# Filler products on TensorE inside the router of a hybrid encoder layer, and the logits moved into the last output tile

## The chip, the cores and the metric

The kernel runs on one core of a Trainium2 chip. Times are device microseconds (us) of one execution; a smaller number is better. The kernel before has a median of 682.71 us over three runs (679.35 to 689.44).

## The reference, cut to what matters

One encoder layer on 512 tokens of width 1024: a mixer of three branches, an output projection with a residual, and then a mixture of experts that is routed in two levels.

```python
merged = gates[:, :, 0] * (o_na @ w_br_na[l]) \
       + gates[:, :, 1] * (o_s5 @ w_br_s5[l]) \
       + gates[:, :, 2] * (o_xa @ w_br_xa[l])
x = x + merged @ w_out[l]                      # the output tiles
h2 = rms_norm(x, norm_ffn[l])
x = x + hierarchical_moe(h2, ...)
...
def hierarchical_moe(h, ...):
    coarse = h @ w_coarse + b_coarse           # 4 groups
    p_coarse = softmax(coarse); grp = top_1(coarse)
    fine = (h @ w_fine + b_fine)               # 16 experts, 4 per group
    fine_g = fine of the chosen group
    top_v, top_i = top_2(fine_g)
    w_top = softmax(top_v) * p_grp
    comb = one_hot(expert_idx) * w_top
    g = h @ w_gate[e]; u = h @ w_up[e]         # 1024 x 256 each
    return sum_e (silu(g) * u * comb[e]) @ w_down[e]
return rms_norm(x, final_norm)
```

All is float32. A wide product is done as three products of float32r halves (hi*hi, lo*hi, hi*lo; the helper `split`, L1477 to L1481).

## The kernel before

Each engine has its own program, written out in order; semaphores join them. The change lies in TensorE's program alone, at the place where the mixer ends and the experts begin.

**Output tiles.** `out_tile(n)` makes 128 tokens times 1024 columns of `merged @ w_out`: 8 chunks of w_out (C_OUT to NCH - 1), two products of depth 128 in each, three matmuls per product, so 48 matmuls of 512 columns. It ends in the semaphore `out_k`. Tiles 0 and 2 write banks 0 and 1, tiles 1 and 3 banks 2 and 3. VectorE adds the residual (L1298, semaphore `x2`), ScalarE takes the sum of squares (L785), and VectorE with ScalarE works out the inverse root (`inverse_root`, L920).

**Turns and logits.** `x2_turn(n)` transposes the tile's 8 blocks into banks 4 and 7. ScalarE copies them out (L791), except for the last tile's second half, which VectorE copies (L1302). `logits(n)` multiplies them by the 20 router columns into bank 5: 8 products that move 20 columns each. TensorE's order is out_tile(0), out_tile(1), x2_turn(0), out_tile(2), x2_turn(1), logits(0), out_tile(3), x2_turn(2), logits(1), logits(2), x2_turn(3), logits(3).

**Router.** After the fourth `logits` VectorE compares the scores (L1315 to L1336) and raises `chosen`. TensorE counts places with small bf16 products (L1781 to L1788, semaphore `places`). VectorE makes one-hot rows for the three first experts (L1357), TensorE turns them into lists of slots (L1793), and VectorE writes the indices (L1366) and `rows` (L1378). The first subtractions of expert weights (L1393) follow on VectorE.

**GpSimd's queue** is in strict order: multiply the last tile of h2 by the norm's gain (L2062) and store it (L2041); gather the tokens of experts 0, 1 and 2 (L2068), once all of h2 is stored; store the last tile of x (L2045); scatter the routing pairs in 8 indirect DMAs (L2083); wait until they have landed; load the lists of slots back (L2087). Then for each expert e: copy its weight (L2091), gather expert e + 3, and add the output of expert e - 1 to the rows of acc_scratch by an indirect DMA (L403, `add_y`). Each `add_y` waits until the one before it has landed. TensorE waits for each expert's gather in `tokens` (L1800).

**SyncE's queue** loads weights. It waits for `out_k` of all four tiles (L493), issues 8 loads of 512 KB, waits for h2's stores, for the four logits and for expert 1's gather (L498 to L500), and goes on; after that each load waits until its buffer is free.

**Experts.** Per expert TensorE does 24 products of 512 columns for gate and up, 2 transposes, 8 transposes of the next expert's tokens, and 12 products for down. ScalarE casts the weights (L821), VectorE subtracts the cast from the weights (L1393), three times per expert. The final norm waits for the last `add_y`.

Of the kernel before, what the change touches and what calls it, by code (L numbers as in the profile page):

```python
# [19 lines left out]
P = 128  # L20
# [20 lines left out]
C_S5G, C_GLU, C_S5P, C_XAG, C_XAP, C_NAG, C_NAP, C_OUT = 20, 26, 29, 31, 39, 41, 49, 53  # L41
NCH = 61
# [74 lines left out]
def build(nc, a, out):  # L117
# [14 lines left out]
    def sem(name):  # L132
        if name not in sems:
            sems[name] = ctx.enter_context(nc.semaphore(name))
        return sems[name]
# [194 lines left out]
    def pv(b, off, *dims, p0=0, pn=P):  # L330
        return v(bank[b], off, *dims, p0=p0, pn=pn)
# [1144 lines left out]
    def _(pe):  # L1476
# [250 lines left out]
                s5_outputs()  # L1727

        def out_tile(n):  # L1730
            for c in range(C_OUT, NCH):
                half, kp = divmod(c - C_OUT, 4)
                if n == 0:
                    pe.wait_ge(sem("w_lo_done"), c + 1)
                h_, l_, o = parts_of(c)
                for kk in range(2):
                    k = 2 * kp + kk
                    if n == 0:
                        pe.wait_ge(sem("m_lo"), k + 1)
                    if k == 0 and n >= 2:  # L1740
                        pe.wait_ge(sem("x2"), n - 1)
                    ins = split(pv(2 * (n % 2) + half, 0, [1, 512]),
                                [v(x, SEQ * k + P * n, [1, P]) for x in (m_hi, m_lo)],
                                [v(w, o + 512 * kk, [1, 512]) for w in (h_, l_)], k == 0, k == KD - 1)
            ins.then_inc(sem("out_k"), 1)

        def x2_turn(n):
            pe.wait_ge(sem("x2"), n + 1)
            for j in range(2):
                if n:  # L1750
                    pe.wait_ge(sem("x2_took"), 2 * n)
                for b in range(4):
                    ins = pe.transpose(pv(H2_BANK[j], P * b, [1, P]), v(x_sb, D * n + P * (4 * j + b), [1, P]),
                                       v(ident, 0, [1, P]))
                ins.then_inc(sem("x2_turned"), 1)

        def logits(n):
            pe.wait_ge(sem("x2_took"), 2 * n + 2)
            for k in range(KD):
                ins = pe.matmul(pv(5, 20 * n, [1, 20]), v(x2T, SEQ * k + P * n, [1, P]), v(wcf, 20 * k, [1, 20]),  # L1760
                                start=k == 0, stop=k == KD - 1)
            ins.then_inc(sem("logits"), 1)
# [7 lines left out]
        x2_turn(1)  # L1770
        pe.wait_ge(sem("wcf_g"), 1)
        logits(0)
        out_tile(3)
        x2_turn(2)
        logits(1)
        logits(2)
        x2_turn(3)
        logits(3)

        pe.wait_ge(sem("chosen"), 1)  # L1780
        pe.matmul(pv(6, 0, [1, 64]), v(upper, 0, [1, P]), v(selb, 0, [1, 64]), start=True, stop=False)  # L1781
# [3 lines left out]
        for n in range(NT):  # L1785
            ins = pe.matmul(pv(6, 64, [1, 16]), v(onesb, 0, [1, P]), v(selb, 16 * n, [1, 16]),
                            start=n == 0, stop=n == NT - 1)
        ins.then_inc(sem("places"), 1)  # L1788

        for e in range(NHOT):  # L1790
            pe.wait_ge(sem("hot"), e + 1)
# [6 lines left out]
        def tokens(e, slot, gathered):  # L1798

            pe.wait_ge(sem(f"xg{slot}"), gathered)  # L1800
            if not (isinstance(e, int) and e == 0):
                pe.wait_ge(sem("xt_lo"), 2 * e)
            for j in range(2):
                for k in range(4):
                    ins = pe.transpose(pv(4 + j, P * k, [1, P]), v(xg, D * slot + 4 * j + k, [KD, P]),  # L1805
                                       v(ident, 0, [1, P]))
                ins.then_inc(sem("xt"), 1)
# [10 lines left out]
        def step(e0, i=None):  # L1818
# [24 lines left out]
            if not first:  # L1843
# [9 lines left out]
                                    [v(w[s3], D * k + 512 * n, [1, 512]) for w in (e_hi, e_lo)], k == 0, k == 1)  # L1853
                ins.then_inc(sem("e_used"), 1)

        pe.wait_ge(sem("rows"), 1)
        tokens(0, 0, 16)
        for e in range(3):
            step(e)
        with pe.Fori(0, 2) as i:  # L1860
# [292 lines left out]
```

## Time and profile before

| | |
|---|---|
| median of three runs | 682.71 us (679.35 to 689.44) |
| profiled execution, its own time | 685.42 us |
| span of its records | 683.5 us |
| mean granted TensorE clock | 0.947 |
| TensorE busy | 609.6 us (89%) |
| VectorE busy | 426.2 us (62%) |
| ScalarE busy | 329.4 us (48%) |
| GpSimd busy | 212.9 us (31%) |
| chain that ended last, share by engine | PE 52%, DMA 23%, DVE 14%, issue 6% |

The profile names the engines PE (TensorE matmuls), PEld (its weight loads), DVE (VectorE), ACT (ScalarE), POOL (GpSimd) and SP (SyncE). Starts are in us from the beginning of the span. L is a line of the kernel. A clock of 1.00 is full speed, 0.50 half of it.

### The profile page before, as it was taken

How to read it: one execution, taken by the hardware profiler on the slowest of the kernel's cores; microseconds unless marked ns; L12 is line 12 of the kernel's file. 1: busy time of each engine (PE TensorE's matmuls, PEld its weight loads, DVE VectorE, ACT ScalarE, POOL GpSimd, SP SyncE). 2: the span in 40 equal slices, each digit the busy share in tenths (PEclk: the TensorE clock that was granted, in tenths of full speed). 3: DMA queues.
4: the chain of work that ended last, by engine and by line, in shares of the span. 5: the costliest groups of instructions: out<-in, count | busy, mean ns of one | idle time of the engine just before them, and what ended most of it. 6: DMA issues, size and time to landing. Idle time of an engine off the chain costs nothing.

```text
span 683.5 us, 9032 instructions
## 1 busy us (share of the span) xinstructions
PE 609.6 (89%) x3173; PEld 490.8 (72%) x3173; DVE 426.2 (62%) x777; ACT 329.4 (48%) x534; POOL 212.9 (31%) x216
## 2 busy tenths in 40 slices
PE   2998999998999999999999997995586999999990
PEld 2787898787877767777778866885475787778770
DVE  4989310586266664555633496325685988988856
ACT  4874422121335333553243264114275888888742
POOL 3509941694000620000000000102823536555620
PEclk9899979999999999999999998996698999999995
DMA  9984322130152322222222338228799999999654
GB/s 298 189 184 119 93 62 59 45 113 1 58 158 62 93 63 61 64 75 79 64 75 78 98 95 304 99 87 307 255 339 357 324 347 372 368 351 359 199 123 185
DMA packets 88336, 113.90 MB, mean 167 GB/s; under 512 B 18246, under 2 KB 65448, under 8 KB 88296
## 3 DMA queue, kind: packets, MB, share of 16 engines
q1 hardware_dynamic: 76776, 93.13, 40.9%
q0 software_dynamic: 6560, 17.55, 10.4%
q10 hardware_dynamic: 4960, 2.70, 1.4%
q8 instruction: 23, 0.38, 0.2%
q14 instruction: 17, 0.14, 0.1%
HBM read 102.08 MB, written 14.75 MB: 171 GB/s over the span
## 4 chain that ended last, share of the span: by engine, by line
PE 52%; DMA 23%; DVE 14%; issue 6%; POOL 2%; ACT 1%; SPq 1%; ACTq 0%; DVEq 0%; POOLq 0%
DMA acc_scratch<-ysb,idx 20%; PE bank L1479 13%; PE bank L1481 13%; PE bank L1480 13%; DVE w_lo L931 3%; PE bank L1654 2%; PE bank L1628 2%; PE bank L1641 2%; PE bank L1554 1%; POOL tok_scratch L2083 1%; PE bank L1589 1%; PE bank L1760 1%; DMA tok_scratch<-pay,rowi 1%; DVE m_lo L1224 1%; PE bank L1565 1%
## 5 line engine op out<-in xcount | busy, mean ns | idle before, releaser
L931 DVE TENSOR_TENSOR w_lo<-raw,w_hi 128x1024 fp32r<-128x1024 f32 x55 | 72.0, 1311 | 119.6 <-ACT w_hi L539 119.2
L1479 PE MATMUL bank<-h_hi,w_hi 128*128 128x512 f32 x320 | 130.3, 407 | 1.6 <-DVE w_lo L931 1.6
L1481 PE MATMUL bank<-h_hi,w_lo 128*128 128x512 f32 x320 | 126.4, 395 | 0.0
L1480 PE MATMUL bank<-h_lo,w_hi 128*128 128x512 f32 x320 | 126.2, 394 | 0.0
L1393 DVE TENSOR_TENSOR e_lo<-eraw,e_hi 128x2048 fp32r<-128x2048 f32 x48 | 108.7, 2288 | 18.3 <-ACT e_hi L821 18.3
L821 ACT CAST e_hi<-eraw 128x2048 fp32r<-128x2048 f32 x48 | 91.8, 1917 | 9.3 <-PE bank L1481 5.5
L539 ACT CAST w_hi<-raw 128x1024 fp32r<-128x1024 f32 x55 | 57.6, 1047 | 29.8 <-PE bank L1481 29.8
L1479 PEld LDWEIGHTS bank<-h_hi,w_hi 128*128 128x128 f32 x320 | 61.3, 192 | 14.1 <-DVE w_lo L931 2.0
L1481 PEld LDWEIGHTS bank<-h_hi,w_lo 128*128 128x128 f32 x320 | 61.0, 191 | 13.4
L1480 PEld LDWEIGHTS bank<-h_lo,w_hi 128*128 128x128 f32 x320 | 61.4, 192 | 11.8
L1479 PE MATMUL bank<-e_hi,xt_hi 128*128 128x512 f32 x128 | 53.6, 419 | 7.3 <-DVE xt_lo L1399 7.3
L2036 POOL TENSOR_TENSOR wcf<-wcf,prt 128x160 f32<-128x160 f32 x1 | 0.5, 455 | 181.9 <-DMA wcf<-in_moe_w_fine 181.9
L1481 PE MATMUL bank<-e_hi,xt_lo 128*128 128x512 f32 x128 | 50.8, 397 | 0.0
L1480 PE MATMUL bank<-e_lo,xt_hi 128*128 128x512 f32 x128 | 50.8, 397 | 0.0
L403 POOL DMA_INDIRECT acc_scratch<-ysb,idx x14 | 28.2, 2014 | 66.6 <-DMA acc_scratch<-ysb,idx 55.5
L637 ACT ACTIVATE gt<-bank,bgh 128x512 f32<-128x512 f32 x24 | 16.5, 690 | 44.6 <-PE bank L1481 44.6
L1479 PEld LDWEIGHTS bank<-e_hi,xt_hi 128*128 128x128 f32 x128 | 24.4, 191 | 17.7 <-issue 7.8
L2068 POOL DMA_INDIRECT xg<-h_scratch,idx x16 | 32.0, 1998 | 8.8 <-DVE idx L1366 6.0
L651 ACT ACTIVATE pr<-ssb,soft 128x192 f32<-128x192 f32 (+1 forms) x32 | 15.2, 475 | 33.0 <-DVE soft L1187 33.0
L1805 PE MATMUL bank<-ident,xg 128*128 128x128 f32 x128 | 18.5, 292 | 11.2 <-DMA xg<-h_scratch,idx 11.2
L1481 PEld LDWEIGHTS bank<-e_hi,xt_lo 128*128 128x128 f32 x128 | 24.5, 191 | 5.4
L1479 PE MATMUL bank<-e_hi,at_hi 128*128 128x512 f32 x64 | 27.2, 424 | 1.1 <-DVE at_lo L1410 1.1
(384 smaller groups left out, 1270.0 us busy)
## 6 DMA issues: line engine op xcount, KB each, us to landing
raw<-in_w_in SPq DMA_DIRECT2D x40, 512.0 KB, 3.8
eraw<-in_moe_w_gate SPq DMA_DIRECT2D x32, 512.0 KB, 9.5
eraw<-in_moe_w_up SPq DMA_DIRECT2D x32, 512.0 KB, 13.4
eraw<-in_moe_w_down SPq DMA_DIRECT2D x32, 512.0 KB, 10.3
raw<-in_w_out SPq DMA_DIRECT2D x8, 512.0 KB, 3.8
x_sb<-in_x SPq DMA_DIRECT2D x4, 512.0 KB, 5.3
raw<-in_w_mem_kv SPq DMA_DIRECT2D x4, 512.0 KB, 8.0
raw<-in_w_br_na SPq DMA_DIRECT2D x4, 512.0 KB, 3.4
```

The source lines that it names most:

```text
L403: pool.indirect_dma_start(out=acc_dram, out_offset=bass.IndirectOffsetOnAxis(ap=v(idx, 2 * e, [1, 1]), axis=0), in_=v(ysb, D * (e % 2), [1 ...
L539: act.copy(v(dst, o, [1, 1024]), v(raw, 1024 * (c % RAW), [1, 1024])).then_inc(sem("w_hi_done"), 1)
L637: ins = act.activation(v(gt, SEQ * m, [1, SEQ]), pv(g % 2, 0, [1, SEQ]), ACT.Tanh, scale=0.5, bias=v(bgh, KD * branch + m, [1, 1]))
L651: ins = act.activation(v(pr, 512 * (p % 2) + 256 * j, [1, n]), src, ACT.Exp, bias=v(soft, so + 1, [1, 1]), accum_out=v(soft, so + 2, [1, 1]))
L821: act.copy(v(e_hi[dst], 0, [1, 2048]), v(eraw, 2048 * j, [1, 2048])).then_inc(sem("e_hi_done"), 1)
L931: dve.tensor_tensor(v(l_, o, [1, 1024]), v(raw, 1024 * (c % RAW), [1, 1024]), raw32(v(h_, o, [1, 1024])), SUB).then_inc(sem("w_lo_done"), 1)
L1393: dve.tensor_tensor(v(e_lo[dst], 0, [1, 2048]), v(eraw, 2048 * j, [1, 2048]), raw32(v(e_hi[dst], 0, [1, 2048])), SUB).then_inc(sem("e_lo_d ...
L1479: pe.matmul(dst, w[0], x[0], start=first, stop=False)
L1480: pe.matmul(dst, w[0], x[1], start=False, stop=False)
L1481: return pe.matmul(dst, w[1], x[0], start=False, stop=last)
L1805: ins = pe.transpose(pv(4 + j, P * k, [1, P]), v(xg, D * slot + 4 * j + k, [KD, P]), v(ident, 0, [1, P]))
L2068: pool.indirect_dma_start(out=v(xg, D * (e % 3), [1, D]), out_offset=None, in_=h2_dram, in_offset=bass.IndirectOffsetOnAxis(ap=rows, axis= ...
```

## The change

A helper `keep_busy(n)` issues n bf16 matmuls of 512 columns; it multiplies two constants (onesb, maskb) into bank 0 and has no semaphore. It is called with 4, 1, 14, 5, 16 and 5: after the last output tile, after its turn, after the last logits, after the places, after the lists of slots, and after the tokens of expert 0. `out_tile` takes a range of chunks, and the third tile's turns and the logits of tiles 1 and 2 stand inside the last output tile, after 3 and after 6 of its 8 chunks.

```diff
-        def out_tile(n):
-            for c in range(C_OUT, NCH):
+        def keep_busy(n):
+
+            for _ in range(n):
+                pe.matmul(pv(0, 0, [1, 512]), v(onesb, 0, [1, P]), v(maskb, 0, [1, 512]), start=True, stop=True)
+
+        def out_tile(n, c0=C_OUT, c1=NCH):
+            for c in range(c0, c1):
                 half, kp = divmod(c - C_OUT, 4)
...
-            ins.then_inc(sem("out_k"), 1)
+            if c1 == NCH:
+                ins.then_inc(sem("out_k"), 1)
...
         x2_turn(1)
         pe.wait_ge(sem("wcf_g"), 1)
         logits(0)
-        out_tile(3)
+        out_tile(3, C_OUT, C_OUT + 3)
         x2_turn(2)
         logits(1)
+        out_tile(3, C_OUT + 3, C_OUT + 6)
         logits(2)
+        out_tile(3, C_OUT + 6)
+        keep_busy(4)
         x2_turn(3)
+        keep_busy(1)
         logits(3)
+        keep_busy(14)
 
         pe.wait_ge(sem("chosen"), 1)
...
         ins.then_inc(sem("places"), 1)
+        keep_busy(5)
 
         for e in range(NHOT):
             pe.wait_ge(sem("hot"), e + 1)
...
+        keep_busy(16)
         pe.wait_ge(sem("rows"), 1)
         tokens(0, 0, 16)
+        keep_busy(5)
         for e in range(3):
             step(e)
```

## Rows read from the trace of the kernel before

**Rows 1.** The chain of waits, in order of time: start, us, what.
```profile
497.17 8.54 DMA tok_scratch<-pay,rowi
514.75 11.17 DMA acc_scratch<-ysb,idx
529.57 11.32 DMA acc_scratch<-ysb,idx
654.48 7.37 DMA acc_scratch<-ysb,idx
```

**Rows 2.** The timeline of PE: start, us, engine, line, operation, idle before.
```profile
461.66 3.65 PE L1760 MATMUL bank<-wcf,x2T 128*128 128x20 f32 x32
467.01 3.52 PE L1760 MATMUL bank<-wcf,x2T 128*128 128x20 f32 x16 [0.78 <-DVE x2T L1302]
474.76 0.23 PE L1781 MATMUL bank<-selb,upper 128*128 128x64 bf16 x1 [4.23 <-DVE selb L1336]
484.24 1.95 PE L1805 MATMUL bank<-ident,xg 128*128 128x128 f32 x8 [4.87 <-DMA xg<-h_scratch,idx]
487.59 0.79 PE L1479 MATMUL bank<-e_hi,xt_hi 128*128 128x512 f32 x1 [1.40 <-DVE xt_lo L1399]
488.60 0.63 PE L1481 MATMUL bank<-e_hi,xt_lo 128*128 128x512 f32 x1
489.03 0.63 PE L1479 MATMUL bank<-e_hi,xt_hi 128*128 128x512 f32 x1
494.55 0.40 PE L1481 MATMUL bank<-e_hi,xt_lo 128*128 128x512 f32 x1
494.78 1.04 PE L1805 MATMUL bank<-ident,xg 128*128 128x128 f32 x8
519.77 1.97 PE L1805 MATMUL bank<-ident,xg 128*128 128x128 f32 x8 [6.36 <-DMA xg<-h_scratch,idx]
```

**Rows 3.** Windows: stretch, length, busy of five engines, clock, DMA share, GB/s.
```profile
467.00:468.00 1.00, 0.99 (x5) 0.99 (x6) 0.56 (x5) 0.20 (x1) 0.00 (x0) 0.56 1.02 418
477.00:479.00 2.00, 0.53 (x8) 0.37 (x8) 1.97 (x13) 2.00 (x2) 0.00 (x0) 0.50 0.02 6
491.00:492.00 1.00, 1.00 (x5) 0.82 (x5) 0.00 (x0) 0.00 (x0) 0.77 (x1) 0.99 1.03 332
```

**Rows 4.** Timelines of DVE, ACT and POOL around the last output tile.
```profile
460.99 1.29 DVE L1298 TENSOR_TENSOR x_sb<-bank,x_sb 128x512 f32<-128x512 f32 x2 [7.95 <-PE bank L1481]
462.38 1.07 ACT L785 ACTIVATE h<-x_sb 128x1024 f32<-128x1024 f32 x1
466.26 0.69 DVE L1302 COPY x2T<-bank 128x512 f32<-128x512 f32 x1 [3.99 <-PE bank L1753]
468.77 1.15 ACT L808 ACTIVATE h<-x_sb,stat 128x1024 f32<-128x1024 f32 x1 [1.52 <-DVEq L1308]
472.64 0.57 POOL L2041 DMA_DIRECT2D h_scratch<-h  x1 [0.30 <-POOL h L2062]
```

**Rows 5.** DMA issues between 472 and 474 us: what, queue, KB, us to landing.
```profile
h_scratch<-h POOLq DMA_DIRECT2D x1, 512.0 KB, 5.2
```

**Rows 6.** Timelines of POOL and DVE between 479 and 500 us.
```profile
479.22 1.12 POOL L2068 DMA_INDIRECT xg<-h_scratch,idx  x1 [6.01 <-DVE idx L1366]
481.83 4.49 DVE L1393 TENSOR_TENSOR e_lo<-eraw,e_hi 128x2048 fp32r<-128x2048 f32 x2
481.98 3.00 POOL L2068 DMA_INDIRECT xg<-h_scratch,idx  x1 [0.30 <-DVE pay L1388]
488.64 2.29 DVE L1393 TENSOR_TENSOR e_lo<-eraw,e_hi 128x2048 fp32r<-128x2048 f32 x1 [1.10 <-ACT e_hi L821]
488.82 2.96 POOL L2083 DMA_INDIRECT tok_scratch<-pay,rowi  x1 [0.30 <-issue]
497.17 0.97 POOL L2083 DMA_INDIRECT tok_scratch<-pay,rowi  x1 [0.30 <-issue]
498.32 2.29 DVE L1393 TENSOR_TENSOR e_lo<-eraw,e_hi 128x2048 fp32r<-128x2048 f32 x1 [0.85 <-ACT e_hi L821]
```

## The prediction, made before the changed kernel was run

> **What bounds the kernel now.** I read the chain of waits backwards from the end. The last part of it is one sequence of 14 indirect adds into acc_scratch, each begun only when the one before has landed, from 514.75 us to the last at 654.48 us [rows 1]. So a gain in the router is worth only what it moves the head of that sequence. The second add, at 529.57 us, waits for expert 1's output, and that stands behind the tokens of expert 3, for which TensorE idled 6.36 us until 519.77 us [rows 2]. That gather cannot be issued before the scattered routing pairs have landed: the last scatter was issued at 497.17 us and took 8.54 us [rows 1]. The path from router to end is therefore: last logits, VectorE's comparisons, GpSimd's gathers and 8 scatters, landing, reload, gather of expert 3. TensorE's matmuls of experts 0 to 2 are not on it; they have the 6.36 us as slack.
>
> Then I read TensorE's clock. It was granted in full until 467 us, fell within the next microsecond (mean 0.56), and was back at 491 us [rows 3]. Before the fall TensorE had done 32 logits products that move 20 columns each and a turn, and then idled 0.78 us; before the rise it had done wide products for some 3.5 us [rows 2]. Half clock is 1.2 GHz, full is 2.4 GHz.
>
> **The change part by part.**
>
> Last tile. In the kernel before, VectorE starts its residual at 460.99 us [rows 4], when the tile's last product is done. Now one turn (8 transposes, busy 1.04 us in the like row of the tokens, an estimated 0.85 to the start of what follows) and two logits (3.65 us busy, an estimated 3.5 to the next start [rows 2]) stand ahead of that point: the residual starts at 465.3 us and ends 1.29 us later, 466.6. The two inputs of the moved logits have long been copied by then, so no wait is added inside the tile. The four fillers lie under the residual: 4 x 0.23 = 0.9 us against 1.3.
>
> Last turn and logits. TensorE turns from 466.7 to 467.6 us. VectorE's copy begins when the 8 transposes are done, at 467.65 us, and ends 0.69 us later, at 468.35. ScalarE's half now stands behind its sum of squares, which in the kernel before was over long before: it starts at 466.65, takes 1.2 us with its read-out, and the copy ends at 468.45. So the logits start at 468.5, not 467.01 us. At full clock they take 1.75 us (half of 3.5 for 32), at half clock 3.52 as measured [rows 2]. I expect full clock, because wide products now stand where the narrow row of logits was: end 470.25 instead of 470.55 us. **Gain 0.3 us**, no more: the 1.8 us from the clock is paid back by the 1.5 us later start.
>
> Fillers in the waits. A filler is priced by the nearest rows, float32r products of the same 512 columns: 0.43 us from start to start at half clock (488.60 to 489.03), 0.23 at full (494.55 to 494.78) [rows 2]. 14 after the logits: 3.2 us under a wait of 4.23 us; at half clock 6.0, which is 1.8 too long. 5 after the places: 1.2 us while VectorE builds the one-hot rows (0 if that covers them, 1.2 if not). 16 after the lists: 3.7 us under the 4.87 us wait for the tokens; at half clock 6.9, 2.0 too long, but that is inside the slack. 5 after the tokens: 1.2 under 1.40. While the clock holds, they cost nothing; their cover is VectorE's comparisons and the gather. The Trainium skill (TensorE: Matmul & The Clock Gate, section "Wait — 56ns, not 53.3ns?") gives 427 and 216 ns for bf16 at the two clocks; by it 14 fillers would take 3.0 us instead of 3.2, and the sum is the same.
>
> Experts 0 to 2. At full clock the first transposes take 1.04 instead of 1.95 us, but VectorE cannot take them before its two subtractions, 481.83 to 486.3 us [rows 6], are done, so gate and up start at 487.3, only the 0.3 earlier. Their 24 products take 24 x 0.23 = 5.5 us instead of 7.19 (487.59 to 494.78) [rows 2]. TensorE is 2.0 us ahead at 492.8 us, and all of it runs into the wait for expert 3. **Gain at the end: none.** The clock falls again in that wait, which no filler covers.
>
> h2 and the loads. VectorE's root needs ScalarE's squares and follows its own copy: copy to scaling is 2.51 us in the kernel before (466.26 to 468.77) [rows 4]. The copy is 1.4 us later, so h2's last store goes out at 474.05 instead of 472.64 us. It landed 5.2 us after issue [rows 5]: 479.25 us, where it was 477.85. The first gather started at 479.22 [rows 6], so h2 now decides it by a little; I take 479.6. SyncE's 8 loads wait for the last tile too and go out at 465.3 instead of 461.0 us. The queues were empty by 477 us [rows 3]; now they are by about 481, so h2's store and the first gather share them. Bounds for the start of the first gather: 0.3 us earlier (the indices decide) to 1.4 us later with some sharing on top. SyncE's next loads hang on expert 1's gather and move with it.
>
> GpSimd against VectorE. An indirect DMA that GpSimd begins after one of VectorE's weight subtractions has begun ends about 0.9 us after the subtraction: the gather at 481.98 took 3.00 us, the scatter at 488.82 took 2.96, where one outside takes 0.97 [rows 6]. The gather at 481.98 us is held in this way already, so 0.4 us of delay ahead of it disappears: it ends with the subtraction in both kernels. But the last scatter, 497.17 us, was just ahead of the subtraction at 498.32 us. That subtraction follows gate and up of expert 0, which are 2.0 us earlier: it begins at 496.3 us, and the last scatter ends at 496.3 + 2.29 + 0.85 = 499.4 instead of 498.14 us. **Loss 1.3 us**, on the path. Bounds: -0.3 (it slips ahead) to 2.0 (a whole hold). I take 1.3.
>
> **Sum:** 685.42 us of the profiled execution + 1.3 = 686.7 us. That execution lies 2.7 us above the median, so the forecast in terms of the median is 684.0 us: no change that can be measured.
>
> **Rivals.**
>
> *No hold.* The 0.3 us reaches GpSimd and the last scatter escapes: 682.71 - 0.3 = 682.4 us. For it: the margin is 0.9 us, and any delay of TensorE widens it. Against it: two holds out of two where the intervals meet. 
> *h2 comes late, the slower side.* If h2's last store lands more than 0.9 us after the point above the first gather needs, the second gather starts after 481.5 us and falls into the first subtraction, the third into the second one. It ends at 486.9 instead of 484.98 us (+1.9), and two of the late scatters fall into the two subtractions after gate and up: the last ends at about 502.5 us, +4.4. That gives 687.1 us. For it: the store goes out 1.4 us later and meets the moved loads. Against it: the store has some 0.4 us left before the indices' own delay.
>
> *The clock does not hold.* The last logits run at half clock (end 472.0, +1.5) and 14 fillers end 1.8 us after `chosen`: +3.3, 686.0 us. Against it: the fillers move 512 columns back to back, as the stretch before the rise did.
>
> *TensorE's gain reaches the end.* If earlier products and weight buffers shorten the adds' sequence, 0.3 + 2.0 us and some of the 0.9 us more saved in the transposes come back: about 3 us, 679.7 us. For it: the sequence's own links vary, from 7.37 to 11.32 us [rows 1], so they leave room for such a gain. Against it: the wait of 6.36 us lies between.
>
> **Chances.** Forecast 0.37, no hold 0.30, h2 late 0.15, TensorE's gain 0.12, clock 0.06. All cases lie within 5 us of 682.71, and 2% is 13.7 us (about what a measurement here can tell from no change). What could carry it past that is only the spread of the runs, 10 us over three: faster 0.02, same 0.95, slower 0.03. The range takes the cases from 682.4 to 687.1, most of the case at 679.7, and 1 us of spread at the upper end: 679.5 to 688.0 us.
>
> **What would show it.** Step 1: residual of the last tile at 465.3, last logits from 468.5 for 1.8 us at clock 1.00. Step 2: clock 1.00 up to the gate products, tokens in 1.04 us. Step 3: h2's last store about 1.4 us later. Step 4: a scatter of nearly 3 us against the subtraction of about 496.3. Step 5: TensorE's wait for expert 3 grows from 6.4 to some 9 us, and its end moves from 519.77 to about 521. Wrong I would be if that wait's end comes before 519, or if the adds' sequence is shorter by more than 2 us.

## The result: a loss of 0.4%, and the profile after

Over 22 runs each, the changed kernel has a median of 685.67 us (681.77 to 693.21) and the kernel before one of 682.90 us (679.35 to 695.08). The ratio is 1.0041 [1.0023, 1.0059], with its 95% interval in brackets: 2.8 us slower, far inside 2%. Every ratio in this document leaves out the executions that fell in the chip's slower state, so it is not exactly the quotient of the medians, which are over all executions. The changed kernel was timed once more later and gave 1.0082 [1.0049, 1.0116]; so one ratio can move by 0.004 from one timing to the next.

The two profiled executions stand the other way round. That of the changed kernel took 681.77 us, the lowest of its 22 runs, and that of the kernel before 685.42 us, above its median. Their ends must not be compared as they are. I compare events by their distance from one event that no part of the change touches: the start of the last output tile's products, 449.78 us before and 447.66 us after. "At 57.9" below means 57.9 us behind that start.

The head of the page of the changed kernel, and its chain's shares:

```profile
span 680.1 us, 9120 instructions
PE 616.9 (91%) x3216; PEld 490.3 (72%) x3218; DVE 427.6 (63%) x777; ACT 329.5 (48%) x534; POOL 216.8 (32%) x216
PE 51%; DMA 22%; DVE 13%; issue 6%; POOL 4%; ACT 2%; SPq 1%; ACTq 0%; DVEq 0%; POOLq 0%
```

TensorE is 7 us busier, and busier on nothing that the output needs. The chain of waits of the changed kernel, in order of time (start, us, what), answers to [rows 1]:

```profile
472.32 7.39 DMA h_scratch<-h
479.76 0.59 issue
...
497.47 8.08 DMA tok_scratch<-pay,rowi
...
514.81 10.89 DMA acc_scratch<-ysb,idx
...
529.58 10.91 DMA acc_scratch<-ysb,idx
...
652.05 6.25 DMA acc_scratch<-ysb,idx
```

The landing of h2's last tile is now a link of the chain, and lasts 7.39 us. The timeline of PE in the changed kernel (start, us, engine, line, operation, idle before), against [rows 2]; L1733 is the filler:

```profile
464.78 1.09 PE L1759 MATMUL bank<-ident,x_sb 128*128 128x128 f32 x8 [0.50 <-DVE x_sb L1298]
466.66 1.96 PE L1766 MATMUL bank<-wcf,x2T 128*128 128x20 f32 x16 [0.57 <-DVE x2T L1302]
468.47 3.18 PE L1733 MATMUL bank<-maskb,onesb 128*128 128x512 bf16 x14
474.09 0.24 PE L1792 MATMUL bank<-selb,upper 128*128 128x64 bf16 x1 [2.44 <-DVE selb L1336]
...
478.56 6.45 PE L1733 MATMUL bank<-maskb,onesb 128*128 128x512 bf16 x16
485.30 1.13 PE L1817 MATMUL bank<-ident,xg 128*128 128x128 f32 x8 [0.28 <-DMA xg<-h_scratch,idx]
...
519.65 1.97 PE L1817 MATMUL bank<-ident,xg 128*128 128x128 f32 x8 [7.50 <-DMA xg<-h_scratch,idx]
```

The last logits run at full clock (1.96 us for 16 products, 3.52 before), and the first tokens too (1.13 against 1.95). The tokens of expert 3 start at 71.99, where they started at 69.99 before: 2.0 us later, after a longer wait. The windows of the changed kernel (stretch, length, busy of PE, PEld, DVE, ACT and POOL, clock, DMA share, GB/s), against [rows 3]:

```profile
471.00:473.00 2.00, 0.65 (x4) 0.10 (x1) 1.97 (x5) 0.00 (x0) 1.59 (x2) 1.00 1.02 414
475.00:477.00 2.00, 1.81 (x8) 0.49 (x6) 1.90 (x12) 1.85 (x2) 0.00 (x0) 0.50 1.02 418
483.00:485.00 2.00, 2.00 (x6) 0.55 (x4) 2.00 (x2) 0.00 (x0) 1.69 (x2) 0.66 0.68 238
```

The clock did fall in the router, to half speed (1.2 GHz), after TensorE had idled 2.44 us for `chosen`; it came back during the 16 fillers, which took 6.45 us. And the DMA queues, which were at a share of 0.02 between 477 and 479 us before [rows 3], are full at 475 to 477 us, which is the same distance behind the last tile's start. The timelines of DVE and POOL in the changed kernel, against [rows 4] and [rows 6]:

```profile
463.44 1.29 DVE L1298 TENSOR_TENSOR x_sb<-bank,x_sb 128x512 f32<-128x512 f32 x2 [12.51 <-PE bank L1481]
468.66 0.68 DVE L1315 SCALAR_TENSOR_TENSOR rt<-bank,stat,lbias 128x20 f32<-128x20 f32 x4 [0.33 <-PE bank L1766]
469.65 2.37 POOL L2076 TENSOR_TENSOR h<-h,gffb 128x1024 f32<-128x1024 f32 x1 [4.51 <-ACT h L808]
469.73 2.37 DVE L1323 TENSOR_TENSOR rt<-rt 128x40 f32<-128x40 f32 x1
472.32 0.57 POOL L2055 DMA_DIRECT2D h_scratch<-h  x1 [0.30 <-POOL h L2076]
480.58 1.12 POOL L2082 DMA_INDIRECT xg<-h_scratch,idx  x1 [7.70 <-DVE idx L1366]
481.03 4.49 DVE L1393 TENSOR_TENSOR e_lo<-eraw,e_hi 128x2048 fp32r<-128x2048 f32 x2
482.01 2.21 POOL L2082 DMA_INDIRECT xg<-h_scratch,idx  x1 [0.30 <-issue]
484.52 1.86 POOL L2082 DMA_INDIRECT xg<-h_scratch,idx  x1 [0.31 <-issue]
497.10 4.50 DVE L1393 TENSOR_TENSOR e_lo<-eraw,e_hi 128x2048 fp32r<-128x2048 f32 x2 [0.85 <-ACT e_hi L821]
497.47 2.77 POOL L2097 DMA_INDIRECT tok_scratch<-pay,rowi  x1 [0.31 <-issue]
```

Two things in it stand in no sum of mine. A comparison of VectorE on 40 columns takes 2.37 us: it begins 0.08 us after GpSimd's multiply of h2 and ends with it. And the first gather starts at 32.92, where it was at 29.44.

SyncE's first load goes out when the last tile ends. Its row in the timeline of SP, in the changed kernel and then in the kernel before:

```profile
463.44 0.33 SPq L473 DMA_DIRECT2D eraw<-in_moe_w_gate  x1
460.98 0.33 SPq L473 DMA_DIRECT2D eraw<-in_moe_w_gate  x1
```

In the table, us from the start of the last tile's products, each from one profiled execution (kernels are explained below; "before, h2 on VectorE" is the best of them):

| | before | after | move only | after, h2 on VectorE | after, loads held | before, h2 on VectorE |
|---|---|---|---|---|---|---|
| last tile's residual starts | 11.21 | 15.78 | 15.78 | 15.78 | 15.78 | 11.21 |
| scores read (L1315) | 20.79 | 21.00 | 21.24 | 21.92 | 21.00 | 20.87 |
| `chosen` written | 24.93 | 26.38 | 26.62 | 25.13 | 26.39 | 24.10 |
| h2's last store issued | 22.86 | 24.66 | 24.64 | 22.30 | 24.66 | 20.52 |
| that store landed | 28.1 | 32.1 | 31.7 | 30.5 | 27.7 | 27.8 |
| first gather | 29.44 | 32.92 | 32.60 | 31.39 | 30.89 | 28.72 |
| last scatter | 47.39 | 49.81 | 50.14 | 48.50 | 48.54 | 46.56 |
| second add | 79.79 | 81.92 | 82.77 | 80.12 | 79.63 | 79.51 |
| last add behind the second | 124.91 | 122.47 | 122.38 | 122.19 | 122.45 | 121.96 |

The start of the first gather follows from two rows of the table: it lies 4.5 us behind `chosen` or some 0.9 us behind the landing of h2's last store, whichever is later, within 0.1 us in all 14 traces of this case. In the kernel before, `chosen` decides (24.93 + 4.5 = 29.4). In the changed kernel `chosen` alone would give 30.9, and the landing gives 32.9. So of the 3.48 us that the first gather lost, 1.45 come from the later `chosen` (0.2 of them from the later scores, the rest from the longer hold of the comparison) and 2.03 from the store.

The last row of the table shows why the profiled execution of before is long: its sequence of adds took 2.4 us more than in the changed kernel's, and 1.9 us or more beyond that of every other kernel I profiled (121.45 to 122.93). No part of any kernel accounts for it. Without that, the changed kernel's second add, 2.1 us later, lies within the interval of the measured 2.8 us (1.6 to 4.0 us). But the second add is a less steady mark than the first gather. In a second profiled execution of the changed kernel (below) the first gather started at 32.90 and the second add at 80.30, only 0.5 us later than before. How much of the 3.48 us reaches the end is therefore not shown by the traces.

### The profile page after: what moved, and what is told of

It reads as the page before. It is cut to its first block, busy times and chain, and to the rows that moved or that the text cites. A ratio compares the mean times of both kernels' runs of the same rounds, so it can differ in the third digit from the quotient of the medians.

```text
span 680.1 us, 9120 instructions
## 1 busy us (share of the span) xinstructions
PE 616.9 (91%) x3216; PEld 490.3 (72%) x3218; DVE 427.6 (63%) x777; ACT 329.5 (48%) x534; POOL 216.8 (32%) x216
## 4 chain that ended last, share of the span: by engine, by line
PE 51%; DMA 22%; DVE 13%; issue 6%; POOL 4%; ACT 2%; SPq 1%; ACTq 0%; DVEq 0%; POOLq 0%
DMA acc_scratch<-ysb,idx 18%; PE bank L1479 13%; PE bank L1481 13%; PE bank L1480 13%; DVE w_lo L931 3%; PE bank L1654 2%; PE bank L1628 2%; PE bank L1641 2%; PE bank L1589 1%; PE bank L1554 1%; DMA tok_scratch<-pay,rowi 1%; POOL tok_scratch L2097 1%; DMA h_scratch<-h 1%; DVE m_lo L1224 1%; PE bank L1565 1%
## 5 line engine op out<-in xcount | busy, mean ns | idle before, releaser
L1393 DVE TENSOR_TENSOR e_lo<-eraw,e_hi 128x2048 fp32r<-128x2048 f32 x48 | 108.8, 2288 | 17.6 <-ACT e_hi L821 17.6
L1480 PEld LDWEIGHTS bank<-h_lo,w_hi 128*128 128x128 f32 x320 | 61.1, 191 | 11.7
L403 POOL DMA_INDIRECT acc_scratch<-ysb,idx x14 | 24.9, 1781 | 61.4 <-DMA acc_scratch<-ysb,idx 49.8
L2082 POOL DMA_INDIRECT xg<-h_scratch,idx x16 | 32.1, 2007 | 10.8 <-DVE idx L1366 7.7
L2105 POOL COPY wcur<-idx 128x1 f32<-128x1 f32 x16 | 26.1, 1633 | 4.9 <-DMA idx<-tok_scratch 4.9
```

The source lines that it names most:

```text
L403: pool.indirect_dma_start(out=acc_dram, out_offset=bass.IndirectOffsetOnAxis(ap=v(idx, 2 * e, [1, 1]), axis=0), in_=v(ysb, D * (e % 2), [1 ...
L1393: dve.tensor_tensor(v(e_lo[dst], 0, [1, 2048]), v(eraw, 2048 * j, [1, 2048]), raw32(v(e_hi[dst], 0, [1, 2048])), SUB).then_inc(sem("e_lo_d ...
L1480: pe.matmul(dst, w[0], x[1], start=False, stop=False)
L2082: pool.indirect_dma_start(out=v(xg, D * (e % 3), [1, D]), out_offset=None, in_=h2_dram, in_offset=bass.IndirectOffsetOnAxis(ap=rows, axis= ...
L2105: pool.tensor_copy(v(wcur, e % 2, [1, 1]), raw32(v(idx, 2 * e + 1, [1, 1]))).then_inc(sem("wcur"), 1)
```

## Experiments

After the result I held three theories. **Move:** the loss comes from the last tile's residual, which is 4.57 us later, by way of GpSimd's queue: h2's store and SyncE's 8 loads. **Fillers:** it comes from the 45 extra products. **Phase:** the fillers change when TensorE's clock falls, in ways that one profiled execution does not show. Every kernel below computes all of the output. Each was timed in 9 or 12 executions, in three groups; the kernel before, timed again beside each group, had medians of 683.16, 682.97 and 682.49 us.

### The move without fillers, the fillers without the move

The first kernel is the changed one without its six calls:

```diff
-        keep_busy(4)
         x2_turn(3)
-        keep_busy(1)
         logits(3)
-        keep_busy(14)
...
```

> The changed kernel without any filler: only the third tile's turns and the logits of tiles 1 and 2 stand inside the last output tile. Theory 1 (the loss lies in GpSimd's queue: the last tile ends 4.6 us later, so h2's last store goes out later and lands among the 8 weight loads that wait for the same tile): the whole loss is here, 685.5 us, ratio to before 1.004; from the start of the last tile's products to the first gather 32.9 us as in the changed kernel, 29.4 in the kernel before. Theory 2 (the fillers cost it: they hold TensorE's queue when the clock is low): no loss here, 682.9 us. Either way the last logits run at full clock if wide products ahead of them are enough, at 3.5 us if the fillers were needed.

Measured: 684.44 us (682.75 to 687.08), ratio 1.0022 [1.0003, 1.0040]. So the move alone is slower than before, by little more than the noise; timed again below it gave 1.0049 [1.0025, 1.0073]. Its last logits took 2.20 us, and its timeline of POOL has the whole pattern: a late first gather, and a second held.

```profile
474.65 0.57 POOL L2049 DMA_DIRECT2D h_scratch<-h  x1 [0.30 <-POOL h L2070]
482.61 1.12 POOL L2076 DMA_INDIRECT xg<-h_scratch,idx  x1 [7.39 <-DVE idx L1366]
484.04 2.78 POOL L2076 DMA_INDIRECT xg<-h_scratch,idx  x1 [0.31 <-DVE pay L1388]
500.15 0.97 POOL L2091 DMA_INDIRECT tok_scratch<-pay,rowi  x1 [0.30 <-issue]
```

Its last scatter, at 500.15 us, is not held: no subtraction was under way when it began. Yet the lists are loaded back at 57.96, against 58.18 in the changed kernel, where that scatter took 2.77 us. A closer pair is the kernel with half of the fillers (below): its last scatter began at 50.18, as late as the 50.14 here, was held for 2.67 us, and the lists came back at 58.49. So the hold on which my sum stood is worth between nothing and 0.5 us in these traces, where I had 1.3.

The second kernel has the order of before, with the fillers; the first four stand ahead of the last turn:

```diff
         out_tile(3)
         x2_turn(2)
         logits(1)
         logits(2)
+        keep_busy(4)
         x2_turn(3)
+        keep_busy(1)
         logits(3)
+        keep_busy(14)
...
```

> The order of the kernel before, with the six groups of fillers (the first four stand ahead of the last turn, behind the logits of tiles 1 and 2). Theory 1: within 0.7 us of before, 682.2 to 683.5 us; the last output tile ends when it did, h2's last store goes out at most 1.1 us later, the first gather at most 1 us later. Theory 2: 685.5 us or more.

Measured: 683.31 us (678.3 to 689.24), ratio 1.0014 [0.9986, 1.0042]: nothing that can be told from no change. In its trace the last logits took 1.96 us, the scores were read at 20.06 (20.79 before), and the first gather began at 29.95 (29.44), in spite of the gain at the scores. It is not h2 that decided this: the store went out at 23.70 instead of 22.86, but landed in 4.2 us, at 27.9. `chosen` did, which came at 25.43 instead of 24.93. The timelines of POOL and DVE show one comparison held for the whole of GpSimd's multiply, as in the changed kernel:

```profile
468.85 2.35 POOL L2074 TENSOR_TENSOR h<-h,gffb 128x1024 f32<-128x1024 f32 x1 [8.14 <-ACT h L808]
468.91 2.37 DVE L1323 TENSOR_TENSOR rt<-rt 128x40 f32<-128x40 f32 x1
```

So the fillers alone lose to this hold what they gain at the logits.

### The route of h2

If the move theory holds, a faster way for h2 must help. In the changed kernel I let VectorE scale the last tile, as it does the other three; ScalarE's scaling (L808) and GpSimd's multiply go:

```diff
-            if n < NT - 1:
-                dve.scalar_tensor_tensor(v(h2, D * n, [1, D]), ..., MUL, MUL).then_inc(sem("h2"), 1)
-        dve.sem_inc(sem("last_root"), 1)
+            dve.scalar_tensor_tensor(v(h2, D * n, [1, D]), ..., MUL, MUL).then_inc(sem("h2"), 1)
...
-        act.activation(v(h2, D * (NT - 1), [1, D]), ...).then_inc(sem("h2_scaled"), 1)
...
-        pool.wait_ge(sem("h2_scaled"), 1)
-        link(pool.tensor_tensor(..., v(gffb, 0, [1, D]), MUL))
+        pool.wait_ge(sem("h2"), NT)
```

> The changed kernel, but h2's last tile is scaled by VectorE in one instruction (1.28 us, as for the other three tiles), in place of ScalarE's scaling and GpSimd's multiply (2.37 us), which held one of VectorE's comparisons for 2.37 us. Theory 1: h2's last store goes out 2.4 us earlier and VectorE's comparisons end about 1 us earlier; the first gather starts at least 2.5 us earlier after the last tile's start (30.4 us or less instead of 32.9), and the time falls by about the same: 683 us, ratio to before 1.000. Theory 2: no gain over the changed kernel, 685.7 us.

Measured: 684.21 us (677.75 to 692.07), ratio 1.0029 [1.0009, 1.0049]. In the trace the store was issued 2.36 us earlier than in the changed kernel, `chosen` came 1.25 us earlier though the scores were read 0.9 us later, and the first gather started 1.5 us earlier. It started no earlier than that because the store, closer behind the loads, now took 8.2 us to land instead of 7.4. The scores were later because VectorE waits only 0.33 us for the logits in the changed kernel, less than its new 1.28 us of work. The interval overlaps that of the changed kernel, so a gain in time is not shown.

The same edit in the kernel before:

> The kernel before, but h2's last tile is scaled by VectorE (1.28 us in the 1.9 us that it waits for the last logits) in place of ScalarE and GpSimd. Theory 1 (GpSimd's queue and VectorE's comparisons are the path): h2's last store 2.4 us earlier, no comparison held by GpSimd's multiply (0.9 us), first gather about 28.5 us after the last tile's start instead of 29.4, time about 682.2 us, ratio 0.9985. Rival (the sequence of adds takes up any shift): 683.1 us, ratio 1.000.

Measured: 680.72 us (677.81 to 685.09), ratio 0.9964 [0.9936, 0.9993]. This is **the best version found**, with the lowest median. It is one timing, its interval overlaps that of `turn first` below, and repeated timings of one kernel moved by 0.003 to 0.004 here; so the gain of 0.4% over the kernel before is likely, not certain. The timelines of DVE and POOL in it:

```profile
467.29 1.28 DVE L1302 SCALAR_TENSOR_TENSOR h<-x_sb,stat,gffb 128x1024 f32<-128x1024 f32 x1
469.94 0.20 DVE L1315 TENSOR_TENSOR rt<-rt 128x20 f32<-128x20 f32 x1
...
468.87 0.56 POOL L2036 DMA_DIRECT2D h_scratch<-h  x1 [7.61 <-DVE h L1302]
477.07 1.17 POOL L2061 DMA_INDIRECT xg<-h_scratch,idx  x1 [7.64 <-DMA h_scratch<-h]
```

VectorE has 1.28 us of new work while it waits for the logits anyway. In return its comparisons meet no multiply of GpSimd's: the first one takes 0.20 us here. In the kernel before the same one took 1.11 us, as its timelines of DVE and POOL show:

```profile
470.00 2.34 POOL L2062 TENSOR_TENSOR h<-h,gffb 128x1024 f32<-128x1024 f32 x1 [7.32 <-ACT h L808]
471.28 1.11 DVE L1320 TENSOR_TENSOR rt<-rt 128x20 f32<-128x20 f32 x1
```

That brings `chosen` 0.83 us forward with scores read at the same point. The first gather gained 0.72: it now waits for the store's landing (27.8), though by little. The store went out 2.34 us earlier than before and landed only 0.3 us earlier, in 7.3 us instead of 5.2.

### The 8 loads

Four of SyncE's eight loads in the changed kernel go behind the landing of h2:

```diff
         load_unit(0, 1, 2)
         load_unit(1, 1, 3)
+        sp.wait_ge(sem("h2_out"), 16 * NT)
         load_unit(2, 0, 4)
         load_unit(0, 2, 5)
-        sp.wait_ge(sem("h2_out"), 16 * NT)
```

> The changed kernel, but SyncE issues 4 of its 8 loads behind the last tile only when h2's last store has landed. Theory 1 (the store lands late because it shares the queues with the 8 loads): it lands in 5 us or less instead of 7.4, so the first gather starts 30.5 to 31 us after the last tile's start instead of 32.9, and the gather of expert 3 some 2 us earlier. The time falls by as much only if the four late loads are not missed: 683.5 to 686 us. If the store's landing does not depend on the loads, the first gather stays at 32.9 us.

Measured: 683.48 us (682.05 to 691.45), ratio 1.0018 [0.9989, 1.0047]. The store of 512 KB, issued at 24.66 as in the changed kernel, landed in 3.0 us. The DMA issues of this kernel (what, queue, KB, us to landing), then its timeline of POOL:

```profile
h_scratch<-h POOLq DMA_DIRECT2D x1, 512.0 KB, 3.0
```

```profile
474.92 0.57 POOL L2055 DMA_DIRECT2D h_scratch<-h  x1 [0.30 <-POOL h L2076]
481.15 1.12 POOL L2082 DMA_INDIRECT xg<-h_scratch,idx  x1 [5.66 <-DVE idx L1366]
482.58 1.03 POOL L2082 DMA_INDIRECT xg<-h_scratch,idx  x1 [0.31 <-issue]
```

The first gather is back at 30.89, 2.03 us ahead of the changed kernel, and the second slips ahead of the subtraction (1.03 us, not 2.21). What made h2's landing late is shown by this: the loads that went out 4.6 us later than before (first of them 15.8 behind the tile's start, 11.2 before) and shared the queues with it. The first gather is still 1.45 us later than in the kernel before, which is what `chosen` is late by. The second add comes at 79.63, 2.3 us ahead of the changed kernel's. The point estimates go the same way (1.0018 against 1.0041), but the intervals overlap, so the gain in time is not proved.

### Holding the clock in the wait for expert 3

TensorE's clock falls in that wait in every kernel so far, and the tokens take 1.97 instead of 1.04 us there, on the path. I put 24 fillers into bank 7 ahead of them in the changed kernel:

```diff
+            if peeled and e == 2:
+                hold_clock(24)
             if not peeled or e < 15:
                 tokens(e + 1, ...)
```

> The changed kernel with 24 more fillers, into bank 7, ahead of the tokens of expert 3, where TensorE waits 7.5 us and its clock falls. Theory 1 (the path runs from GpSimd's gather of expert 3 through TensorE's tokens and expert 1's down product to the second add): tokens at full clock take 1.04 instead of 1.97 us and 12 down products 2.8 instead of 4.7 us, so the second add starts 2 to 2.8 us earlier after the gather of expert 3, and the time is 683.3 us, ratio to before 1.001. A rival: the sequence of adds is set by its own links and by the DMA queues, and the time stays at 685.7 us.

Measured: 683.73 us (680.86 to 693.46), ratio 1.0024 [0.9996, 1.0052]. The timeline of PE in it shows a miss:

```profile
511.36 5.35 PE L1824 MATMUL bank<-maskb,onesb 128*128 128x512 bf16 x24
519.62 1.97 PE L1817 MATMUL bank<-ident,xg 128*128 128x128 f32 x8 [2.91 <-DMA xg<-h_scratch,idx]
```

The fillers were over 2.91 us too soon, the clock fell, and nothing is learned of what a held clock is worth. Two more kernels started from the best version. The first only turns the last tile ahead of the two waiting logits:

```diff
         out_tile(3)
         x2_turn(2)
+        x2_turn(3)
         logits(1)
         logits(2)
-        x2_turn(3)
         logits(3)
```

> The kernel before with VectorE scaling h2's last tile and one change of order: the last tile's turn goes ahead of the logits of tiles 1 and 2, which then lie under the copies, and nothing is moved into the last output tile. Theory 1: the last tile's end stays at 11.2 us after its start; last logits end 1 to 2 us earlier than in the kernel before (19 to 20 us instead of 20.8), h2's last store at about 18 us instead of 22.9, first gather at 26.5 us instead of 29.4, time 680 to 681 us, ratio 0.996. Rival: no gain, 1.000.

Measured: 682.02 us (680.41 to 693.45), ratio 0.9976 [0.9956, 0.9997]. All 48 logits products now stand in one row of 7.07 us, and the scores were read at 20.87, exactly as without the edit. The clock fell 17.6 us behind the tile's start, as without it, so the second half of that row ran at half clock. h2's store did go out 2.5 us earlier (18.00) and landed at 26.1, but the first gather, at 28.60, gained only 0.12: with the store out of the way, `chosen` decides it. The second adds 28 fillers ahead of the tokens of expert 3:

> The same with 28 fillers into bank 7 ahead of the tokens of expert 3. If the fillers end within half a microsecond of the tokens' arrival, the clock holds there and the tokens and 12 down products take 2.8 us less, on the path: 677.5 to 678.5 us, ratio 0.993. Rival: the sequence of adds is set by its own links, and fillers on the path are worth nothing either: as without them, 0.996.

Measured: 681.73 us (676.32 to 689.13), ratio 1.0005 [0.9974, 1.0036]. In its timeline of PE (one filler has no record) the clock held:

```profile
511.68 5.99 PE L1807 MATMUL bank<-maskb,onesb 128*128 128x512 bf16 x27
517.51 1.13 PE L1800 MATMUL bank<-ident,xg 128*128 128x128 f32 x8
```

The tokens took 1.13 us, and the second add came at 76.55, against 79.39 without the fillers. The tokens started at 69.2 in both, so this is the whole gain of a held clock in the tokens and in the products behind them, 2.8 us as expected. Its profiled execution was the shortest of all kernels, 676.32 us. But the median is only 0.3 us below that of the kernel without them, and the ratios say nothing clearer. I had expected both.

### Are the fillers themselves dear?

To ask whether fillers cost something that a profiled execution does not show, I ran the changed kernel and the move without fillers again, together on one chip, and between them the changed kernel with 2, 1, 7, 2, 8 and 2 fillers.

> The changed kernel once more, beside the next three on one chip. If its ratio is that of the kernel: 1.002 to 1.006. Theory 3 (new: the fillers raise the median although their traces look better, since the clock falls at another point of the router in each execution, and 14 fillers at 0.43 us end up to 1.8 us after VectorE's choice): higher than without fillers by 0.001 to 0.003.

> The move without fillers once more. Theory 3: 0.001 to 0.003 below the changed kernel of this job, near 1.002. If the fillers cost nothing, the two are level.

```diff
-        keep_busy(4)
+        keep_busy(2)
...
-        keep_busy(14)
+        keep_busy(7)
...
-        keep_busy(16)
+        keep_busy(8)
...
```

> The changed kernel with half the fillers (2, 1, 7, 2, 8, 2): at half clock 7 take 3.0 us, which VectorE's 4 to 5 us of comparisons cover at any clock. Theory 3: back to the level of the move alone, 1.002, with a narrower spread of runs than with all fillers. If the fillers cost nothing: level with the changed kernel.

Measured: changed kernel 686.59 us (680.53 to 693.47, 9 runs), ratio 1.0082 [1.0049, 1.0116]; without fillers 684.65 (682.37 to 690.2), 1.0049 [1.0025, 1.0073]; with half of them 685.5 (682.4 to 687.61), 1.0042 [1.0015, 1.0068]. The order of the first two is the one that dear fillers would give, but the intervals overlap, and the half is level with none. Each kernel's ratio is also 0.003 to 0.004 above its own first one (1.0041 and 1.0022).

All runs together say more. For each kernel I set its profiled execution against the median of its own runs:

| kernel | fillers | profiled | median | difference |
|---|---|---|---|---|
| changed | 45 | 681.77 | 685.67 | -3.9 |
| changed, again | 45 | 680.53 | 686.59 | -6.1 |
| fillers alone | 45 | 678.30 | 683.31 | -5.0 |
| changed, h2 on VectorE | 45 | 677.75 | 684.21 | -6.5 |
| changed, 24 more fillers | 69 | 680.86 | 683.73 | -2.9 |
| changed, loads held | 45 | 682.56 | 683.48 | -0.9 |
| turn first, 28 fillers | 28 | 676.32 | 681.73 | -5.4 |
| half of the fillers | 22 | 685.71 | 685.50 | +0.2 |
| move alone, twice | 0 | 684.81, 682.37 | 684.44, 684.65 | +0.4, -2.3 |
| before, h2 on VectorE | 0 | 679.91 | 680.72 | -0.8 |
| turn first | 0 | 680.65 | 682.02 | -1.4 |
| half of the move (below) | 0 | 683.58 | 682.33 | +1.3 |
| before | 0 | 685.42 | 682.90 | +2.5 |

With 28 or more fillers the profiled execution lies 0.9 to 6.5 us below the median, on average 4.4; without fillers, or with half, between 2.3 below and 2.5 above, on average level. In six of the seven kernels with 28 or more fillers the profiled execution is the lowest of its runs. So a profiled execution of a kernel full of fillers is not like its other runs, and shows them too good.

What the other executions do in the router, no trace shows. But each of them has its mean granted clock on record, and that answers a part. In the changed kernel it is 0.964 on average over the executions without a trace, 0.961 in the one with it, and 0.953 in the kernel before, timed beside it when it was run again. So the fillers did raise the clock in every execution and not in the profiled one alone, and the time did not follow. That fits a clock gain in a stretch that waits anyway. Why the profiled executions are the short ones stays open.

### Half of the move

The last kernel joins the best version with half of the move: the third tile's turn and logits(1) inside the last output tile, logits(2) behind it, no fillers.

```diff
-        out_tile(3)
+        out_tile(3, C_OUT, C_OUT + 3)
         x2_turn(2)
         logits(1)
+        out_tile(3, C_OUT + 3)
         logits(2)
         x2_turn(3)
         logits(3)
```

> The kernel before with VectorE scaling h2's last tile, no filler, and only the third tile's turn and the logits of tile 1 inside the last output tile; the logits of tile 2 stand behind the tile, under its residual (1.75 us against 1.3). Last tile's end 13.8 us after its start (11.2 before, 15.8 changed), last logits done at about 19 us if the clock holds, VectorE's scores from 19.9 us instead of 20.8, h2's last store about 20 us, first gather 28 to 28.5 us. Theory 1: level with or up to 0.7 us better than the kernel before with VectorE scaling, 680 to 681 us, ratio 0.9955. If the late loads spoil it as in the changed kernel: 0.999 or more.

Measured: 682.33 us (680.56 to 691.96), ratio 1.0012 [0.9982, 1.0041]. Its `chosen` was the earliest of all kernels (23.41, 24.10 in the best version). But the last tile's residual, and with it the loads, came 2.7 us later than before, and the timeline of POOL shows what it cost:

```profile
469.88 0.56 POOL L2043 DMA_DIRECT2D h_scratch<-h  x1 [4.95 <-DVE h L1302]
478.76 1.11 POOL L2068 DMA_INDIRECT xg<-h_scratch,idx  x1 [8.33 <-DVE idx L1361]
480.18 2.71 POOL L2068 DMA_INDIRECT xg<-h_scratch,idx  x1 [0.30 <-issue]
```

The store needed 8 us to land, and the first gather started at 29.46, 0.74 us later than in the best version. Even with h2 ready early, the move loses by the loads what it gains in the logits: `chosen` alone would have let the gather start at 27.9. Not tried: this kernel, or the best version, with half of the loads held.

## Why the prediction was right, and where it was not

The forecast was 684.0 us and no measurable change; measured were 685.67 us, and 2.8 us more than the kernel before against my 1.3. That the number came near is partly luck: its one term, the hold of the last scatter, was worth at most 0.5 us of my 1.3, and the delays that arose stood at little or nothing in the sum. The direction, the small size and the path by GpSimd's queue to the wait for expert 3 were right. The steps:

**Last tile and logits (step 1): right, but for its last 0.5 us.** The residual moved by 4.57 us (forecast 4.3), the last logits ran at full clock. They started at 19.00 and took 1.96 us, not 1.75. So the scores were read 0.2 us later, where I had 0.3 earlier. Of the gain in clock, the late start ate all.

**Clock and fillers (step 2): half right.** The clock was full for the last logits, but it fell behind the 14 fillers, in the wait for `chosen`, which is longer than I had it because `chosen` was late. All the same nothing was lost by it: the 14 fillers ended before `chosen`, and the 16 fillers, which took 6.45 us at mixed clock, ended 0.28 us before the tokens could start. The rival "the clock does not hold" did not happen as priced.

**Comparisons: missed.** The sum holds nothing for VectorE's comparisons. GpSimd's multiply now begins as they begin, and holds one of them for 2.37 us; in the kernel before it was half over and held one for 1.11 us. `chosen` moved by 1.45 us in place of -0.3. I had used this interference in one direction only, VectorE against GpSimd's DMAs, and not asked what the later multiply of GpSimd would meet on VectorE. The best version shows it: with the multiply gone, the comparison takes 0.20 us.

**h2 and the loads (step 3): mis-sized; this is where the forecast failed.** I had the store 1.4 us later and landing in 5.2 us as before [rows 5]; it was 1.8 us later, and landed in 7.39. The first gather moved by 3.5 us where I took 0.4 and bounded it at 1.4 "with some sharing on top". Of that, 1.45 us are the late `chosen` of the last paragraph; the other 2.03 are the late landing. I also let the gather start 0.35 us behind the landing, where it takes 0.9. In the landing the sharing is the larger part: held loads bring it to 3.0 us. The rival "h2 comes late" is what happened: the second gather was held (2.21 us), the third too (1.86). I gave it 0.15, because the store seemed to have 0.4 us left; I had counted the landing time as a constant of the transfer, when it is one of the traffic beside it. Its price of 4.4 us was about twice what came: the second add moved 2.1 us in the one execution and 0.5 in the other.

**The hold of the last scatter (step 4): it came, but for another reason, and it is worth little.** The scatter took 2.77 us, held by a subtraction. I had that subtraction 2.0 us earlier than before and the scatter in its place. Measured from the last tile's start, the subtraction began at 49.44, which is 0.9 us later than before (48.54; my forecast was 46.5), and the scatter was 2.4 us late (49.81, 47.39 before) and so ran into it. TensorE was not ahead: the tokens of expert 0 started 3.2 us late behind the late gathers. And without the hold, in the move alone, the lists come back at 57.96, with it at 58.18 and, in the kernel with half of the fillers, at 58.49. The 1.3 us of my sum is at most 0.5; the true terms are the comparison and the store.

The Trainium skill (SBUF — State Buffer, section "Who interferes with whom") says that a probe saw tensor_tensor not stall DMAs. By that there would be no hold. Here the measurement decides: every indirect DMA that began inside a subtraction was held, in every trace, and ended some 0.9 us behind it; a direct store of GpSimd's, 0.57 to 0.59 us, never was.

**Wait for expert 3 (step 5): right in direction.** It grew from 6.36 to 7.50 us, not to some 9, because TensorE, which I had 2.0 us ahead, came to it 0.9 us later than before (64.49, 63.63 before): the faster products made up only part of the late tokens. Its end moved by 2.0 us, and by 1.1 in the second execution (forecast 1.2 us, from 69.99 to 71.2). TensorE's own gain did end in it.

**The rest.** Why the fillers' kernels have medians above their profiled executions is open. So the division of the 2.8 us between move and fillers is not shown: the move alone measured 1.5 us (ratio 1.0022 [1.0003, 1.0040]) and 3.3 us (1.0049 [1.0025, 1.0073]), which can be all of it. That the move costs time is shown by both timings. That it does so by the comparison and the store is shown for the start of the first gather, by the traces, and only argued for the time: no version of the changed kernel that eased one of the two or both was clear of the changed kernel's interval.

## What to carry to other kernels

Before an instruction is put ahead of a semaphore, list all that hangs on it, in other queues too: here the loads were the dear part, by making another transfer's landing 2 us longer. Issuing that transfer earlier brings less than it seems, as long as it stays behind the same loads: 2.34 us earlier in the best version, landed 0.3 us earlier. A fill of a wait that is not on the path buys a faster clock for work that waits anyway. And a small operation can be cheaper on the engine that idles (VectorE's 1.28 us) than on one whose work holds the critical engine.

Compare medians, and use one profiled execution for the mechanism only: here its end misplaced a kernel by up to 6.5 us, more than any effect studied. And time a kernel twice before an effect of 0.4% is believed: repeats moved by as much.

## What the runs showed of the hardware that I had not expected

- GpSimd's tensor_tensor on 1024 columns holds a VectorE tensor_tensor on 20 or 40 columns until it ends: 1.11 and 2.37 us in place of about 0.2.
- The same 512 KB store landed in 3.0 us with four of the eight loads held back, and otherwise the faster the longer it was issued behind the first of them: 8.0 to 8.2 us at a distance of 6.5 to 6.8 us, 7.1 to 7.4 at 8.9 to 9.3, 5.2 at 11.7 (the kernel before) and 4.2 at 12.5 (the fillers alone).
- 14 bf16 products of 512 columns took 3.18 us at full clock, and 4.87 us in the kernel with fillers alone, where the clock was low for part of them.
- The clock's low stretch in the router moved from 17 to 41 us behind the last tile's start (before) to 26.5 to 36.5 (changed kernel) and 27 to 34 (the same kernel again): fillers shorten it, and did not remove it.
